# Latent queries of a two-layer block in three fp32r products, with five small moves of neighbouring work

## The chip, the cores and the metric

The kernel runs on one core of one Trainium2 chip, in one launch. The metric is the device time of one execution in microseconds (us). Three runs of the kernel before gave 2176.4, 2179.35 and 2181.2 us, so 2179.35 us in the median.

A core has TensorE (PE, matrix products, with its weight loads shown as PEld), VectorE (DVE), ScalarE (ACT), GpSimd (POOL) and SyncE (SP), which here only issues the DMA transfers. Each engine works through its own list in order, and the engines wait for each other by semaphores. Nothing is reordered at run time: an instruction that waits holds up all that stands behind it on its engine.

## The reference, cut to what matters

The program computes two transformer layers on 512 tokens of 1024 features. The parts that the change touches are these:

```python
x = x + rms_norm(mixed, post_norm_gain)                      # layer 1: a sum of squares over 1024 features ("post")
...
n = rmsnorm(h, norm_mix)                                     # layer 2: "mix", 528 tokens (16 more in front)
c_q = ...n @ w_in[:, 0:384]                                  # latent of the queries
q = (rmsnorm(c_q, q_norm) @ w_uq)                            # 384 -> 8 heads * (128 + 64): the latent queries
...
h = h + mix @ w_out
peer_ffn(rmsnorm(h, norm_ffn), ...)                          # "ffn"
    q = (h @ w_q);  s = q . sub_keys; top-k of 128 + 128 keys, 8 heads
    out[t] = sum over 16384 experts e of gate[t, e] * gelu(h[t] . u[e]) * v[e]
```

The expert layer is computed densely: all 16384 experts for all tokens, with a table of gates that is zero except for the chosen ones.

## The kernel before, in words

Features lie on the partitions and tokens along the free dimension, in tiles of 128 features by 512 tokens. A product is one of two kinds. **fp32 products** (`project`, line 791; sums of squares in `sums`, 884, and `big_sums`, 901) take the fp32 operands as they are; the trace shows each as two matmul records. **fp32r products** (`three`, lines 802 to 804) split both operands into an upper part, rounded to fp32r, and a lower part, the rest, and add up*up + up*low + low*up: three matmul records.

Weights come by DMA in chunks of up to 128x2048 into a ring of four slots of `wring`; the list WEIGHTS gives their order, and its last field says whether a chunk is to be split. POOL does the splitting (`split_group`): CASTs of 128x512 for the upper part (line 2577, one of two slots behind the ring) and subtractions for the lower part (line 2581, in place). It takes the chunks in the order of the list, waits for a chunk to land, and waits until the products of the chunk two places earlier in the list of split ones have released their upper slot. The order on each engine is written out by hand.

**Sums of squares.** For "post", "mix" and "ffn" ACT squares pairs of tiles, DVE adds the two tiles of a pair (`add_squares`, line 2002), and PE multiplies each of the four pair sums by a matrix of ones (line 901).

**Latent queries.** PE computes c_q, c_kv and k_pe, then 12 tiles of queries with 3 products of 128x512 each (`project_part`), in groups between sums of squares of earlier parts. The chunks are uqn0, uqn1 and uqp, 128x1536 each, not split.

**Expert scores and top-k.** For each of 8 heads PE computes the query (`query(h)`, weights pq0 to pq7) and then the scores (`ps`, line 1377), one head ahead. DVE finds the top-k (`best16`); POOL weighs the one-hot places (`weigh_places`, line 2613), DVE sums them. For pq6 and pq7 ACT does the rounding (line 1852), and POOL only the subtraction.

**First expert stage** (u). 128 tiles of 128 experts. A tile of 512 KB lands in one of six slots of `wring`; ACT rounds it (`round_u`, 1856), POOL makes the rest (`split_u`, 2621), PE does 16 products (1386, 1387), ACT takes the gelu (1878). ACT rounds tile t+4 behind the gelu of tile t. Beside tiles 44 to 111 the gate table is made in 128 quads: DVE makes one-hots (2494, 2495), ACT and POOL weigh them (1888, 2643), PE multiplies (1412, 1413) into PSUM, and DVE copies 128x512 to a stage (2504), from which SP stores the pieces to `gate_table`.

**Second expert stage** (v). 64 steps: ACT rounds v (`round_v`, 1893), DVE makes its rest (2509), DVE multiplies hidden values by gates (2519), ACT rounds these coefficients (1899), DVE makes their rest (2525), PE does 32 products (1438, 1439).

Of the kernel before, what the change touches and what calls it, by code (L numbers as in the profile page):

```python
# [80 lines left out]
USLOT = (1, 2, 3, 5, 0, 4)  # L81
# [39 lines left out]
for _name, _n in (("pre", 8), ("mix", 8), ("subln", 1), ("conv", 12), ("post", 8), ("ple", 8), ("qnorm", 3),  # L121
# [179 lines left out]

ADDED = ["post", "mix", "ffn"]


def build(nc, A):
    ctx = ExitStack()
    with ctx:
# [87 lines left out]
        cq = view(15488, 3, T)  # L395
        ckv = view(17024, 2, TM)
# [118 lines left out]
        x2_ready = sem("x2_ready")  # L515
        roped = sem("roped")
# [109 lines left out]
        def _(sp):  # L626
# [90 lines left out]
            for t in range(TILES):  # L717
# [13 lines left out]
                if t == TILES - len(USLOT) - 1:  # L731
# [3 lines left out]
                    load_v(1)  # L735

# [29 lines left out]
        def _(pe):  # L766
# [121 lines left out]
            def big_sums(name, width=T, pairs=range(4)):  # L888
# [5 lines left out]
                for m in pairs:  # L894
                    if name in ADDED:
                        pe.wait_ge(pair_added, 4 * ADDED.index(name) + m + 1)
                    else:
                        pe.wait_ge(squares, 4 * BIG.index(name) + m + 1)
                    for k in (2 * m,) if name in ADDED else (2 * m, 2 * m + 1):
                        for at, n in ((0, T), (T, META)) if width == TM else ((0, T),):  # L900
                            mm = pe.matmul(flat(key)[:, at:at + n], ones, sq[:, k, at:at + n],
                                           start=(k == 0), stop=(m == 3 and k == (6 if name in ADDED else 7)))
# [197 lines left out]

            def project_part(name):
                kind, m = name[0:2], int(name[2:])
                if kind == "qn":
                    if m == 0:
                        pe.wait_ge(normed, NORM["cq"] + 1)
                    project(("uqn", m), f"uqn{m // 2}", (2 * (m % 2), 2 * (m % 2) + 1), cq, 3)
                elif kind == "qp":
                    project(("uqp", m), "uqp", (2 * m, 2 * m + 1), cq, 3)
# [354 lines left out]
        def _(act):  # L1463
# [185 lines left out]
            square("ckv", norm_sq("ckv")[:, 0:2 * TM].rearrange("p (k t) -> p k t", k=2), ckv)  # L1649
            when_filled(act, ("kpe", 0))  # L1650
# [208 lines left out]
            for h in range(HP):  # L1859
                if h + 1 < HP:  # L1860
                    query(h + 1)
                copy_out(("ps", h), sc[:, h].rearrange("p a b -> p (a b)"), flat(("ps", h)))
                if h == HP - 2:
                    round_u(0)
                    round_u(1)
# [60 lines left out]
            for g in range(BEFORE + BESIDE, GROUPS):  # L1926
                for j in range(EG):
                    gelu(g, j)
                    beside(EG * g + j)
                    if g >= GROUPS - 2 and j % 2:  # L1930
                        if (g, j) == (GROUPS - 2, 1):
                            act.wait_ge(stored[1], 8 * PIECES * STORES)
                        round_v(2 * (g + 2 - GROUPS) + j // 2)
            for n in range(2):
                round_coefs(n)
            round_coefs(2)
# [861 lines left out]
```

## Time and profile before

| what | value |
|---|---|
| median of three runs | 2179.35 us (2176.4 to 2181.2) |
| the profiled execution's own time | 2177.73 us |
| its span, first to last instruction | 2175.9 us |
| PE busy | 2115.4 us, 97% |
| DVE, ACT, POOL busy | 1304.1, 922.6 and 1033.5 us |
| mean granted TensorE clock | 0.992 |

How to read it: the times below are those of the profiled execution, counted from the span's start; 1.8 us of its time lie outside the span. A matmul record lasts longer than the step to the next one because matmuls are pipelined; the step from start to start is what a product takes in a row of products.

### The profile page before, as it was taken

What the parts mean: (1) busy time and instruction counts of PE and PEld (TensorE: products, weight loads), DVE (VectorE), ACT (ScalarE), POOL (GpSimd) and SP (SyncE); (2) the same over time, 40 slices, a digit from 0 to 9 for tenths busy, and PEclk for the clock granted to TensorE, in tenths of its full rate; (3) what the DMA queues carried; (4) which work ended last, traced back from release to release, by engine and by line L of the source; (5) the groups of instructions that cost most, each with busy time, mean ns of one, the idle gap of its engine ahead of it and who ended that gap; (6) DMA issues with size and microseconds to landing.
All of it is one profiled execution on the core that took longest, in us unless ns stands there. A gap on an engine that the chain in (4) does not pass through costs nothing.

```text
span 2175.9 us, 27394 instructions
## 1 busy us (share of the span) xinstructions
PE 2115.4 (97%) x10296; PEld 1661.6 (76%) x10296; DVE 1304.1 (60%) x2244; ACT 922.6 (42%) x1528; POOL 1033.5 (47%) x892
## 2 busy tenths in 40 slices
PE   8999999999999999999999998999999899999999
PEld 6877767557887776887878877777778788888887
DVE  6456257352235774215898957888881666666664
ACT  4223343572234234111334447777773434343432
POOL 6655546212324122877859887999996100000000
PEclk9999999999999999999999999999999999999999
DMA  5222312201111111233216664777788988888884
GB/s 201 100 78 78 116 61 90 90 30 49 59 40 59 59 55 43 97 122 110 78 59 199 205 206 141 272 289 246 272 291 294 333 300 286 289 284 300 288 287 149
DMA packets 98291, 359.32 MB, mean 165 GB/s; under 512 B 8480, under 2 KB 41504, under 8 KB 73328
## 3 DMA queue, kind: packets, MB, share of 16 engines
q1 hardware_dynamic: 98160, 357.56, 47.3%
q8 instruction: 83, 1.36, 0.3%
q14 instruction: 48, 0.39, 0.1%
HBM read 286.09 MB, written 71.30 MB: 164 GB/s over the span
## 4 chain that ended last, share of the span: by engine, by line
PE 67%; POOL 13%; DVE 11%; issue 6%; ACT 2%; DMA 1%; POOLq 0%; SPq 0%; ACTq 0%; DVEq 0%
PE ps L1438 11%; PE ps L1439 11%; PE ps L802 10%; PE ps L803 9%; PE ps L804 9%; POOL area L2643 6%; POOL wring_parts L2621 6%; PE ps L791 2%; PE ps L1249 2%; DVE area L2413 2%; PE ps L1386 1%; PE ps L1387 1%; DVE area L2410 1%; PE ps L884 1%; PE ps L1225 1%
## 5 line engine op out<-in xcount | busy, mean ns | idle before, releaser
L2577 POOL CAST wring_parts<-wring 128x512 fp32r<-128x512 f32 x236 | 170.5, 764 | 546.0 <-PE ps L804 429.3
L1386 PE MATMUL ps<-sqbuf_parts,wring_parts 128*128 128x512 f32 x1024 | 412.6, 403 | 5.5 <-POOL wring_parts L2621 5.5
L1387 PE MATMUL ps<-normed_x_parts,wring_parts 128*128 128x512 f32 x1024 | 404.4, 395 | 0.0
L2621 POOL TENSOR_TENSOR wring_parts<-wring_parts,wring 128x512 fp32r<-128x512 f32 x256 | 331.0, 1323 | 76.0 <-ACT wring_parts L1856 73.0
L2581 POOL TENSOR_TENSOR wring_parts<-wring,wring_parts 128x512 fp32r<-128x512 f32 x244 | 351.2, 1470 | 6.6 <-ACT wring_parts L1852 1.5
L1386 PEld LDWEIGHTS ps<-sqbuf_parts,wring_parts 128*128 128x128 f32 x1024 | 194.0, 189 | 50.6 <-POOL wring_parts L2621 4.9
L1387 PEld LDWEIGHTS ps<-normed_x_parts,wring_parts 128*128 128x128 f32 x1024 | 193.9, 189 | 41.8
L802 PE MATMUL ps<-resid_parts,wring_parts 128*128 128x512 f32 (+1 forms) x528 | 201.2, 381 | 6.1 <-DVE normed_x_parts L2010 3.3
L803 PE MATMUL ps<-normed_x_parts,wring_parts 128*128 128x512 f32 (+1 forms) x528 | 197.0, 373 | 0.0
L804 PE MATMUL ps<-resid_parts,wring_parts 128*128 128x512 f32 (+1 forms) x528 | 196.2, 372 | 0.0
L1474 ACT ACTIVATE area<-ps 128x1024 f32<-128x1024 f32 (+6 forms) x89 | 61.7, 696 | 275.2 <-PE ps L804 183.5
L2504 DVE COPY area<-ps 128x512 f32<-128x512 f32 x128 | 138.9, 1087 | 56.3 <-PE ps L1413 56.3
L803 PE MATMUL ps<-area_parts,wring_parts 128*128 128x512 f32 x440 | 172.4, 392 | 0.0
L1888 ACT ACTIVATE area<-area,rt 128x128 bf16<-128x128 bf16 x512 | 156.5, 390 | 3.7 <-DVE area L2494 3.7
L1878 ACT ACTIVATE area<-ps 128x512 f32<-128x512 f32 x128 | 76.3, 597 | 187.0 <-PE ps L1387 187.0
L802 PE MATMUL ps<-area_parts,wring_parts 128*128 128x512 f32 x376 | 150.1, 399 | 4.8 <-POOL wring_parts L2581 2.3
L804 PE MATMUL ps<-area_parts,wring_parts 128*128 128x512 f32 x376 | 146.7, 390 | 0.0
L1438 PE MATMUL ps<-cst_parts,area_parts 128*128 128x512 f32 x352 | 138.3, 393 | 4.7 <-issue 4.7
L1439 PE MATMUL ps<-rt_parts,area_parts 128*128 128x512 f32 x352 | 138.0, 392 | 0.0
L1856 ACT ACTIVATE wring_parts<-wring 128x1024 fp32r<-128x1024 f32 x128 | 134.4, 1052 | 7.2 <-DMA wring<-in_uT_dram 7.2
L1438 PE MATMUL ps<-normed_x_parts,area_parts 128*128 128x512 f32 x352 | 136.9, 389 | 0.0
L1439 PE MATMUL ps<-normed_x_parts,area_parts 128*128 128x512 f32 x352 | 136.9, 389 | 0.0
(269 smaller groups left out, 4431.4 us busy)
## 6 DMA issues: line engine op xcount, KB each, us to landing
wring<-in_weights_dram SPq DMA_DIRECT2D x65, 1024.0 KB, 4.8
wring<-in_uT_dram SPq DMA_DIRECT2D x128, 512.0 KB, 4.4
area<-in_vT_dram SPq DMA_DIRECT2D x44, 1024.0 KB, 7.2
hidden_table<-area SPq DMA_DIRECT2D x32, 1024.0 KB, 6.7
gate_table<-area SPq DMA_DIRECT2D x32, 1024.0 KB, 8.4
area<-gate_table SPq DMA_DIRECT2D x32, 1024.0 KB, 9.1
wring<-in_vT_dram SPq DMA_DIRECT2D x20, 1024.0 KB, 6.7
rt<-hidden_table SPq DMA_DIRECT2D x32, 512.0 KB, 4.6
```

The lines of the kernel that those rows point to most:

```text
L802: pe.matmul(out, a_up, b_up, start=first, stop=False)
L803: pe.matmul(out, a_up, b_low, start=False, stop=False)
L804: return pe.matmul(out, a_low, b_up, start=False, stop=last)
L1386: pe.matmul(out, first[:, d], h_first[:, k, :], start=(k == 0), stop=False)
L1387: mm = pe.matmul(out, rest[:, d], h_rest[:, k, :], start=False, stop=(k == KD - 1))
L1438: pe.matmul(out, v_first[:, j, d], c_first[:, t], start=(n == 0 and j == 0), stop=False)
L1439: mm = pe.matmul(out, v_rest[:, j, d], c_rest[:, t], start=False, stop=(n == HALVES - 1 and j == 1))
L1888: ins = act.activation(gateB[:, q, i, 0, :], oneB[:, q, i, :], ACT.Copy, scale=entT[:, 2, t:t + 1])
L2504: dve.tensor_copy(dst[:, 4 * i:4 * i + 4, :], spread_out(n)).then_inc(copied, 1)
L2577: ins = nc.gpsimd.tensor_copy(up[:, d, :], W(name)[:, d, :])
L2581: ins = nc.gpsimd.tensor_tensor(low[:, d, :], W(name)[:, d, :], up[:, d, :], ALU.subtract)
L2621: ins = nc.gpsimd.tensor_tensor(rest[:, a:a + PIECE], first[:, a:a + PIECE], u_raw[t % len(USLOT)][:, a:a + PIECE], ALU.subtract)
```

## The change

Six edits.

1. The chunks uqn0, uqn1 and uqp are split, so POOL gets nine CASTs and nine subtractions of 128x512 more. ACT rounds the normed latent c_q (128x1536) and DVE subtracts, and the 36 fp32 products of the queries become 108 fp32r products. As the list of split chunks is three longer, the upper slots swap, and the order of the u slots (USLOT) follows.
2. DVE adds the sums of the first three pairs into one tile, so that "post", "mix" and "ffn" need two products with ones in place of four. DVE gets two additions more for each.
3. The copy of a quad (line 2504) goes through the same elements in another order: it reads PSUM at a step of 128 elements and writes runs of four.
4. ACT rounds the u tiles 0 and 1 ahead of taking out the last query, and POOL splits them ahead of `weigh_places(1)` and of the subtraction of pq7; POOL splits tiles 2 and 3 ahead of `weigh_places(2)`, as before.
5. The loads of v 0 and 1 stand at tile 116 in place of 121.
6. ACT rounds v 2 and 3 behind the first two coefficients in place of between the last gelus, and DVE makes the rest of coefficient 1 ahead of v 2 and 3.

```diff
-USLOT = (1, 2, 3, 5, 0, 4)
+USLOT = (1, 2, 3, 4, 0, 5)
-              ("kpe0", 8, 128, True), ("uqn0", 3, 512, False), ("uqn1", 3, 512, False), ("uqp", 3, 512, False),
+              ("kpe0", 8, 128, True), ("uqn0", 3, 512, True), ("uqn1", 3, 512, True), ("uqp", 3, 512, True),
 ADDED = ["post", "mix", "ffn"]
+ADDED_TILES = ((), (), (4,), (6,))
...
-                if t == TILES - len(USLOT) - 1:
+                if t == EG * (BEFORE + BESIDE) + 4:
                     sp.wait_ge(stored[0], 8 * PIECES * STORES)
                     load_v(0)
                     load_v(1)
+                if t == TILES - len(USLOT) - 1:
...
                     if name in ADDED:
-                        pe.wait_ge(pair_added, 4 * ADDED.index(name) + m + 1)
+                        if m >= 2:
+                            pe.wait_ge(pair_added, 2 * ADDED.index(name) + m - 1)
...
+            def project_query(key, name, tiles):
+                claim(key)
+                up, low = split_arrived(name)
+                for a, m in enumerate(tiles):
+                    d = slice(m * P, (m + 1) * P)
+                    for k in range(3):
+                        mm = three(pair(key)[:, a, :], (up[:, k, d], low[:, k, d]),
+                                   (CQ_PARTS[0][:, k, :], CQ_PARTS[1][:, k, :]), k == 0, k == 2)
+                fills(mm, key)
...
-                        pe.wait_ge(normed, NORM["cq"] + 1)
-                    project(("uqn", m), f"uqn{m // 2}", (2 * (m % 2), 2 * (m % 2) + 1), cq, 3)
+                        pe.wait_ge(latent_low, 1)
+                    project_query(("uqn", m), f"uqn{m // 2}", (2 * (m % 2), 2 * (m % 2) + 1))
...
             square("ckv", norm_sq("ckv")[:, 0:2 * TM].rearrange("p (k t) -> p k t", k=2), ckv)
+            act.wait_ge(normed, NORM["cq"] + 1)
+            act.activation(CQ_PARTS[0], cq, ACT.Copy).then_inc(latent_up, 1)
...
             for h in range(HP):
+                if h == HP - 2:
+                    round_u(0)
+                    round_u(1)
                 if h + 1 < HP:
                     query(h + 1)
                 copy_out(("ps", h), sc[:, h].rearrange("p a b -> p (a b)"), flat(("ps", h)))
-                if h == HP - 2:
-                    round_u(0)
-                    round_u(1)
...
-                    if g >= GROUPS - 2 and j % 2:
-                        if (g, j) == (GROUPS - 2, 1):
-                            act.wait_ge(stored[1], 8 * PIECES * STORES)
-                        round_v(2 * (g + 2 - GROUPS) + j // 2)
+                    if g == GROUPS - 2 and j % 2:
+                        round_v(j // 2)
             for n in range(2):
                 round_coefs(n)
+            act.wait_ge(stored[1], 8 * PIECES * STORES)
+            round_v(2)
+            round_v(3)
...
-                dve.tensor_tensor(sq[:, 2 * m, :], sq[:, 2 * m, :], sq[:, 2 * m + 1, :], ALU.add).then_inc(pair_added, 1)
+                ins = dve.tensor_tensor(sq[:, 2 * m, :], sq[:, 2 * m, :], sq[:, 2 * m + 1, :], ALU.add)
+                if m in (1, 2):
+                    link(ins)
+                    ins = dve.tensor_tensor(sq[:, 2 * m, :], sq[:, 2 * m, :], sq[:, 2 * m - 2, :], ALU.add)
+                if m < 2:
+                    link(ins)
+                    return
+                ins.then_inc(pair_added, 1)
...
+            dve.wait_ge(latent_up, 1)
+            dve.tensor_tensor(CQ_PARTS[1], cq, CQ_PARTS[0], ALU.subtract).then_inc(latent_low, 1)
...
-                dst = stage[:, piece % 2, :].rearrange("p (j t) -> p t j", t=HALF)
+                dst = stage[:, piece % 2, :].rearrange("p (j t) -> p j t", t=HALF)
                 dve.wait_ge(spread, n + 1)
-                dve.tensor_copy(dst[:, 4 * i:4 * i + 4, :], spread_out(n)).then_inc(copied, 1)
+                dve.tensor_copy(dst[:, :, 4 * i:4 * i + 4], spread_out(n).rearrange("p t n -> p n t")).then_inc(copied, 1)
...
             split_coefs(0)
+            split_coefs(1)
             split_v(2)
             split_v(3)
-            split_coefs(1)
...
             for h in range(HP):
-                if h == 2:
-                    for split in range(4):
+                if h in (1, 2):
+                    for split in range(2 * h - 2, 2 * h):
                         split_u(split)
                 weigh_places(h)
```

Three places show how instructions move. Line numbers of the changed kernel are some 5 to 31 higher. First POOL, at the end of the weight chunks: 2613 and 2644 are `weigh_places`, 2581 and 2612 the subtraction of a query chunk (pq6, then pq7), 2621 and 2652 `split_u`. Before:

```order
L2613 TENSOR_TENSOR area<-area 128x1024 [waits places_hot] x2
L2581 TENSOR_TENSOR wring_parts<-wring,wring_parts 128x512 [waits query_up,filled0,w_in3]
L2581 TENSOR_TENSOR wring_parts<-wring,wring_parts 128x512 x3
L2613 TENSOR_TENSOR area<-area 128x1024 [waits places_hot] x2
L2581 TENSOR_TENSOR wring_parts<-wring,wring_parts 128x512 [waits query_up,filled2,w_in0]
L2581 TENSOR_TENSOR wring_parts<-wring,wring_parts 128x512 x3
L2621 TENSOR_TENSOR wring_parts<-wring_parts,wring 128x512 [waits u_rounded]
L2621 TENSOR_TENSOR wring_parts<-wring_parts,wring 128x512
```

And of the change:

```order
L2644 TENSOR_TENSOR area<-area 128x1024 [waits places_hot] x2
L2612 TENSOR_TENSOR wring_parts<-wring,wring_parts 128x512 [waits query_up,filled0,w_in3]
L2612 TENSOR_TENSOR wring_parts<-wring,wring_parts 128x512 x3
L2652 TENSOR_TENSOR wring_parts<-wring_parts,wring 128x512 [waits u_rounded]
L2652 TENSOR_TENSOR wring_parts<-wring_parts,wring 128x512
L2652 TENSOR_TENSOR wring_parts<-wring_parts,wring 128x512 [waits u_rounded]
L2652 TENSOR_TENSOR wring_parts<-wring_parts,wring 128x512
L2644 TENSOR_TENSOR area<-area 128x1024 [waits places_hot] x2
L2612 TENSOR_TENSOR wring_parts<-wring,wring_parts 128x512 [waits query_up,filled2,w_in0]
L2612 TENSOR_TENSOR wring_parts<-wring,wring_parts 128x512 x3
```

Two `split_u`, each waiting for ACT's rounding, now stand ahead of `weigh_places(1)` and pq7.

Second ACT at the same place: 1474 and 1493 are copies out of PSUM (query 6, scores 5, query 7, scores 6, scores 7), 1856 and 1877 `round_u`. Before:

```order
L1474 ACTIVATE area<-ps 128x1024 [waits filled0,filled3]
L1474 ACTIVATE area<-ps 128x1024 [waits filled1]
L1474 ACTIVATE area<-ps 128x1024 [waits filled2,filled1]
L1474 ACTIVATE area<-ps 128x1024 [waits filled3]
L1856 ACTIVATE wring_parts<-wring 128x1024 [waits u_in0]
L1856 ACTIVATE wring_parts<-wring 128x1024 [waits u_in1]
L1474 ACTIVATE area<-ps 128x1024 [waits filled0]
```

And of the change:

```order
L1493 ACTIVATE area<-ps 128x1024 [waits filled0,filled3]
L1493 ACTIVATE area<-ps 128x1024 [waits filled1]
L1877 ACTIVATE wring_parts<-wring 128x1024 [waits u_in0]
L1877 ACTIVATE wring_parts<-wring 128x1024 [waits u_in1]
L1493 ACTIVATE area<-ps 128x1024 [waits filled2,filled1]
L1493 ACTIVATE area<-ps 128x1024 [waits filled3]
L1493 ACTIVATE area<-ps 128x1024 [waits filled0]
```

The two roundings moved up by two copies and still stand behind the copy of scores 5.

Third the transfers that SP issues near the end of the first expert stage. Before:

```order
L680 DMA hidden_table<-area 128x2048 [waits gelu_done]
L676 DMA wring<-in_uT_dram 128x1024 [waits pre_done] x4
L680 DMA hidden_table<-area 128x2048 [waits gelu_done]
L676 DMA wring<-in_uT_dram 128x1024 [waits pre_done]
L694 DMA area<-in_vT_dram 128x2048 [waits stored0]
L694 DMA area<-in_vT_dram 128x2048
L700 DMA area<-gate_table 128x8x256 [waits spread,stored1]
```

And of the change:

```order
L685 DMA hidden_table<-area 128x2048 [waits gelu_done]
L699 DMA area<-in_vT_dram 128x2048 [waits stored0]
L699 DMA area<-in_vT_dram 128x2048
L681 DMA wring<-in_uT_dram 128x1024 [waits pre_done] x4
L685 DMA hidden_table<-area 128x2048 [waits gelu_done]
L681 DMA wring<-in_uT_dram 128x1024 [waits pre_done]
L705 DMA area<-gate_table 128x8x256 [waits spread,stored1]
```

The two loads of v, 1 MB each, now stand ahead of the last five u tiles (123 to 127).

## Rows read from the trace of the kernel before

**Rows 1.** The page, part 1: busy us, share of span, instructions.
```profile
PE 2115.4 (97%) x10296; PEld 1661.6 (76%) x10296; DVE 1304.1 (60%) x2244; ACT 922.6 (42%) x1528; POOL 1033.5 (47%) x892
```
**Rows 2.** Waits of PE, longest first: us in total, times, longest us.
```profile
PE ps L1412 <- POOL area L2643: 10.4, 26, 2.4
PE ps L1386 <- POOL wring_parts L2621: 5.5, 5, 2.9
```
**Rows 3.** Timeline of PE, an fp32r stretch: start us, us, engine and line.
```profile
235.18 0.39 PE L804 MATMUL ps<-area_parts,wring_parts 128*128 128x512 f32 x1
...
244.28 0.39 PE L804 MATMUL ps<-area_parts,wring_parts 128*128 128x512 f32 x1
```
**Rows 4.** Chain that ended last, latent queries: start us, us, what.
```profile
397.39 5.15 PE ps L791 x12
...
403.62 15.65 PE ps L791 x36
```
**Rows 5.** Timeline of ACT and POOL ahead of the latent queries.
```profile
390.50 1.09 ACT L1482 ACTIVATE sqbuf<-area 128x1056 f32<-128x1056 f32 x1
381.47 1.17 POOL L2577 CAST wring_parts<-wring 128x512 fp32r<-128x512 f32 x2 [6.17 <-PE ps L804]
```
**Rows 6.** Timeline of DVE in "mix": the same subtraction beside POOL and alone.
```profile
343.95 2.31 DVE L1984 TENSOR_TENSOR area_parts<-area,area_parts 128x1024 fp32r<-128x1024 f32 x1
354.82 1.23 DVE L1984 TENSOR_TENSOR area_parts<-area,area_parts 128x1024 fp32r<-128x1024 f32 x1 [0.51 <-ACT area_parts L1508]
```
**Rows 7.** Timeline of PE, products with ones in post, mix, ffn.
```profile
281.64 3.60 PE L901 MATMUL ps<-sqbuf,cst 128*128 128x512 f32 x8
354.37 1.25 PE L901 MATMUL ps<-sqbuf,cst 128*128 128x512 f32 x4 [1.08 <-DVE sqbuf L2002]
1033.23 1.02 PE L901 MATMUL ps<-sqbuf,cst 128*128 128x512 f32 x2
```
**Rows 8.** Windows of PE: length, busy (instructions), PEclk, DMA share, GB/s.
```profile
986.30:990.30 4.00, 2.17 (x10) 1.00 0.05 20
444.60:448.60 4.00, 2.04 (x7) 0.87 0.00 0
1137.30:1145.30 8.00, 8.00 (x29) 0.80 0.19 52
1145.30:1153.30 8.00, 8.00 (x36) 1.00 0.47 147
```
**Rows 9.** Timeline of ACT, PE, POOL around query 7 and tile 0.
```profile
1118.55 1.02 ACT L1474 ACTIVATE area<-ps 128x1024 f32<-128x1024 f32 x1 [0.70 <-PE ps L1377]
1119.61 0.47 PE L802 MATMUL ps<-area_parts,wring_parts 128*128 128x512 f32 x1 [1.09 <-POOL wring_parts L2581]
1137.29 0.76 PE L1386 MATMUL ps<-sqbuf_parts,wring_parts 128*128 128x512 f32 x1 [2.94 <-POOL wring_parts L2621]
```
**Rows 10.** Timeline of POOL in the same stage.
```profile
1088.27 4.73 POOL L2613 TENSOR_TENSOR area<-area 128x1024 f32<-128x1024 f32 x2
1094.47 5.03 POOL L2581 TENSOR_TENSOR wring_parts<-wring,wring_parts 128x512 fp32r<-128x512 f32 x4 [1.47 <-ACT wring_parts L1852]
1134.64 9.98 POOL L2621 TENSOR_TENSOR wring_parts<-wring_parts,wring 128x512 fp32r<-128x512 f32 x8 [15.17 <-ACT wring_parts L1856]
```
**Rows 11.** Line 2504: min/median/max ns, first and last start.
```profile
L2504 DVE COPY area<-ps x128: 1001/1086/1115, 1313.8 to 1641.1; 128x512 f32<-128x512 f32 x128
```
**Rows 12.** Waits of DVE from 1340 to 1640 us.
```profile
DVE area L2504 <- PE ps L1413: 45.3, 62, 2.0
```
**Rows 13.** Timeline of ACT, PE and DVE, end of the first expert stage.
```profile
1670.99 1.06 ACT L1856 ACTIVATE wring_parts<-wring 128x1024 fp32r<-128x1024 f32 x1
1678.14 8.20 DMA area<-in_vT_dram
1706.36 0.76 PE L1438 MATMUL ps<-cst_parts,area_parts 128*128 128x512 f32 x1 [4.74 <-issue]
1705.04 1.23 DVE L2525 SCALAR_TENSOR_TENSOR rt_parts<-cst_parts,rt 128x1024 fp32r<-128x1024 f32 x1 [5.08 <-ACT cst_parts L1899]
```

More of the change, by code:

```diff
@@ L395, in build @@
         cq = view(15488, 3, T)
+        CQ_PARTS = [area_parts[:, at:at + 3 * T].rearrange("p (k t) -> p k t", k=3) for at in (10368, 15488)]
         ckv = view(17024, 2, TM)
@@ L515, in build @@
         x2_ready = sem("x2_ready")
+        latent_up = sem("latent_up")
+        latent_low = sem("latent_low")
         roped = sem("roped")
@@ L895, in big_sums @@
                     if name in ADDED:
-                        pe.wait_ge(pair_added, 4 * ADDED.index(name) + m + 1)
+                        if m >= 2:
+                            pe.wait_ge(pair_added, 2 * ADDED.index(name) + m - 1)
                     else:
                         pe.wait_ge(squares, 4 * BIG.index(name) + m + 1)
-                    for k in (2 * m,) if name in ADDED else (2 * m, 2 * m + 1):
+                    for k in ADDED_TILES[m] if name in ADDED else (2 * m, 2 * m + 1):
                         for at, n in ((0, T), (T, META)) if width == TM else ((0, T),):
                             mm = pe.matmul(flat(key)[:, at:at + n], ones, sq[:, k, at:at + n],
-                                           start=(k == 0), stop=(m == 3 and k == (6 if name in ADDED else 7)))
+                                           start=(k == ADDED_TILES[2][0] if name in ADDED else k == 0),
+                                           stop=(k == ADDED_TILES[3][0] if name in ADDED else k == KD - 1))
                 if pairs[-1] == 3:
@@ L1104, in project_part @@
                     if m == 0:
-                        pe.wait_ge(normed, NORM["cq"] + 1)
-                    project(("uqn", m), f"uqn{m // 2}", (2 * (m % 2), 2 * (m % 2) + 1), cq, 3)
+                        pe.wait_ge(latent_low, 1)
+                    project_query(("uqn", m), f"uqn{m // 2}", (2 * (m % 2), 2 * (m % 2) + 1))
                 elif kind == "qp":
-                    project(("uqp", m), "uqp", (2 * m, 2 * m + 1), cq, 3)
+                    project_query(("uqp", m), "uqp", (2 * m, 2 * m + 1))
                 else:
```

## The prediction, made before the change was run

> **What bounds the kernel now.** I read the page's first part, then the waits of PE, then the timeline of each stage that the diff touches. PE is busy 97% of a span of 2175.9 us [rows 1], so an edit shows in the time only where it shortens PE's own work or one of its few waits, or makes a new wait. In the list of waits the reader is to see how little there is to win: the largest entry is 10.4 us in 26 pieces behind POOL's weighing of one-hots, the next 5.5 us behind the splitting of u [rows 2]. The timelines then tell, per edit, whether PE waits there, and for which instruction. A second thing to watch is the granted clock. After 1.83 us without work PE kept full clock, and after 1.96 us and 2.94 us it did not (0.87 and 0.80 in the windows behind) [rows 8, 9]. The full-clock window of 8 us holds 36 products, the one behind the 2.94 us holds 29 [rows 8]: 7 to 8 products of 0.23 us, about 1.7 us lost. So a wait of over about 2 us costs itself and some 1.7 us more, and a wait that gets shorter than that gives both back.
>
> **The sums of squares** (edit 2). In "post" eight records (four products) take 3.60 us, the last one's pipelined end included [rows 7], so 0.86 us each. PE does not wait there, and two products go: -1.7. DVE's two added adds (0.7 us each by the size of such adds, my estimate) lie beside earlier products. In "mix" two products of about 1.1 us (1.25 with the pipelined end) [rows 7] go too, but PE already waited 1.08 us for DVE's add of the last pair before 354.37. That add comes no earlier, so the 2.1 us turn into idle time, 3.2 us in all, which passes the 2 us after which the clock fell: no gain and one half-clock episode, +1.6, between 0 and +1.8. In "ffn" the last product stands at 1033.23 [rows 7]; the addition that it needs ends about 0.6 us before, so it can move up by 0.5: -0.5, between -1.7 and 0.
>
> **The latent queries** (edit 1). 36 records of fp32 take 15.65 us [rows 4]; two records are a product, so a product takes 0.869 us. An fp32r product in three records: from 235.18 to 244.28 the stretch holds 13 of them, 9.10 us [rows 3], 0.700 each. 36 products: 36 x 0.169 is -6.1, with the same from a second stretch -6.2. What must be ready in time: PE reaches the first of them at 397.39 [rows 4]. ACT is free at 391.59 [rows 5] and takes about 1.5 us for 128x1536 (1.09 for 1056), so 393.1. DVE's subtraction of 1024 columns took 2.31 us beside POOL and 1.23 alone [rows 6]; for 1536 that is 1.8 to 3.5, so 394.9 to 396.6. POOL casts at 0.58 us and subtracts at 1.25 us per 512 [rows 5, 10], 5.5 us for a chunk of 1536; free from 389.8 on, it would have the first chunk at about 396.5 at the latest, the second at 402, the third at 412 to 414, where PE wants them at 397, 407 and 420. So covered, with a slack under a microsecond for the first: -6.2, at worst -5.2 (1 us of wait). If POOL were wholly late by a chunk's 5.5 us, -0.7; I don't take that as an end since it was idle 6.17 us in that place [rows 5].
>
> **The order around query 7** (edit 4). This is the term that decides. Before, POOL did `weigh_places(1)` (4.73 us) and the subtraction of pq7 (5.03 us) [rows 10] while PE did scores 5, and PE waited only 1.09 us for it before query 7 at 1119.61 [rows 9]. Now two `split_u` stand ahead of both, and each waits for a rounding that ACT does behind its copy of scores 5. That copy starts only when PE has finished scores 5, at 1118.55, and ends at 1119.57 [rows 9]. So POOL is held from about 1100 to: round_u(0) done 1120.6; splits 0 and 1, 2 x 2.5 (9.98 us for four tiles [rows 10]), 1125.6; weigh_places 4.73, 1130.3; subtraction 5.03, 1135.4; query 7 at about 1135.6. PE has nothing else in its order: +16.0. Behind 17 us of idle it runs at half clock, +1.7. Given back: tiles 0 and 1 are split early, so the wait of 2.94 us before tile 0 [rows 9] becomes about 1.15 us (now for ACT's copy of the last scores), -1.8, and no half clock there, -1.6. DVE's top-k chain behind `weigh_places(1)` is late by only some 9.7 us against PE's 16, so POOL's weighing in the stage after, on which PE waits in small pieces [rows 2], is earlier against PE by about 6 us; some 1.3 us of these waits lie in its first part and I take them off. Sum: 16.0 + 1.7 - 1.8 - 1.6 - 1.3 = +13.0, between +11 and +17.
>
> **The end of the first expert stage** (edits 5 and 6). Before, the load of v 0 was issued at 1678.14 and took 8.20 us [rows 13]; ACT, which rounds v 0 between the last gelus, stood still for it, PE waited about 1.1 us in two pieces behind that, and its second stage then started at 1706.36 after 4.74 us without work, for DVE's rest of the coefficient (1.23 us, ending 1706.27) [rows 13]. With v 0 early, the first stage ends 1.1 to 1.7 us sooner, and ACT goes straight from the last gelu to the coefficients; its 5.08 us ahead of DVE [rows 13] shrink to the rounding itself. I get coefficients at 1701.5, their rest at 1702.9, the second stage at 1703: -3.4, with 3.1 us still idle, so the half clock stays. Lower end -1 (only the 1.1 us). The price could be in the u tiles 123 to 127, issued behind these 2 MB. At the 400 GB/s of a full queue (1 MB in some 2.6 us, my estimate; a queue's share alone was 8.20 us [rows 13]) they come about 5.2 us later; tile 123 was rounded at 1670.99 [rows 13] and PE reads it only some 10 us later, so 1.2 us of slack are left by my count. I take 0 for it.
>
> **The quad copy** (edit 3). It takes 1.086 us now, 128 times [rows 11]. DVE was idle 45.3 us at just these copies, waiting for PE [rows 12]: over some 118 quads 0.38 us each, so a copy of up to 1.47 us costs nothing, and a faster one gains nothing unless it loosens a wait of PE. The new access is in no row. Bounds: 0.61 us (the 1.225 us that other copies out of PSUM take for 1024, halved, my estimate) and twice the present, 2.17 us. The old copy goes through one side at a wide step already, the new one through the other, so I take the present value: 0.
> The Trainium skill, page "PSUM — Partial Sum Buffer", section "Specifications (TRN2)", gives PSUM lines of 8 bytes and says that patterns that are not contiguous slow access; "SBUF — State Buffer", section "Specifications (TRN2)", gives SBUF lines of 16 bytes of which two hits are wanted. By the first the new read is worse, by the second the new write of four fp32 in a row is better. No row here tells which wins.
>
> **Sum** over the profiled execution: -1.7 + 1.6 - 6.2 - 0.5 + 13.0 - 3.4 = +2.8, rounded up for the wait that may be left before the first query: +3.0, so 2177.7 + 3.0 = 2180.7. The profiled execution lies 1.6 us below the median of the runs; on the median it is 2182.4.
>
> **Rivals.**
> (a) Slower, the copy. Reading PSUM at a step of 128 elements costs DVE more than the 0.38 us of slack. It decides from 1.47 us on; at 2.17 us each quad sets the pace, (2.17 - 1.47) x 128 = +90, about 2270. For it: never seen here. Against it: a copy that reads in order and writes at a step costs 1.09 already.
> (b) Slower, the loads. The two v loads hold the five u tiles for the 8.20 us that one took in rows 13, not for 5.2: PE waits about 4.3 us for tile 123 and pays a half clock: +6, about 2188. For it: 8.20 us is the only duration of such a load in the rows. Against it: two loads were issued together there, beside u tiles. Of each SDMA engine the Trainium skill ("DMA: Bandwidth & Descriptors", section "Queues, rings and completion order") says that it takes descriptors in ring order, which would make the u tiles wait whole; the order on SP alone shows that too.
> (c) Faster, no hole. POOL or ACT get to tiles 0 and 1 early by a way that I have overlooked, and query 7 is not held. Then the waits before tile 0 go and nothing comes: -6.8 - 3.4 - 3.4 = -13.6 or a bit less, 2166. For it: ACT and POOL each have stretches without work in this stage, so the work itself would fit. Against it: the waits in the order leave no other way.
> (d) Faster copy. At 0.6 us, DVE releases PSUM and the stage earlier and some of the 10.4 us behind POOL [rows 2] go: +3.0 - 7 to 8, about 2175.
> (e) The clock is kinder: no episode in "mix", none behind the hole, and the one behind 1.96 us at 444.6 goes: 3.0 - 5, about 2177.
>
> **Chances.** Forecast 0.60, its own range 2178 to 2187; (a) 0.07, (b) 0.10, (c) 0.07, (d) 0.08, (e) 0.08. A measurement of this kernel can't tell under 0.2% from no change, that is 4.4 us, 2175.0 to 2183.7. Faster: (c) 0.07, half of (d) 0.04, 0.02 of the forecast and of (e) 0.01, so 0.14. Slower: (a) 0.07, (b) 0.07, the forecast 0.27: 0.41. Same: 0.45. The range goes down past (d) and up past (b), 2171 to 2191; it leaves out (a) and (c), 0.14, and tails.
>
> **What would show it.** PE idle of about 16 us before query 7, its releaser POOL's subtraction, and POOL idle ahead of a `split_u` that waits for ACT; no wait of PE at 397; the query stretch 25 us long, not 31; PE idle 3 us before the last product of "mix"; tile 0 started behind ACT; the second expert stage some 3 us earlier against the end of the first; the quad copy's mean under 1.4 us. I am wrong if query 7 is not late, if the copy's mean passes 1.47 us, or if PE waits for u tiles 123 to 127.

## The result: 0.2% slower, and the trace of the kernel after

| | before | after |
|---|---|---|
| median of 22 runs each | 2177.62 us | 2182.46 us |
| ratio of after to before | | 1.0022, 95% interval 1.0014 to 1.0029 |
| profiled execution: time, span | 2177.73, 2175.9 us | 2182.15, 2180.4 us |

The forecast was 2182.4 us with a difference of +3.0 us; measured were 2182.46 us and +4.8 us. That the time itself was hit to 0.1 us is luck in part: the three runs of before that I had lay 1.7 us above the median of 22, and the difference was 1.8 us too small.

I cut both profiled executions at PE instructions that stand in both (a start is the time in the timeline of PE) and compare the lengths of the pieces:

| piece, by its start in before | before, us | after, us | difference | forecast |
|---|---|---|---|---|
| up to 199.8 (nothing changed) | 199.82 | 199.23 | -0.6 | 0 |
| to 324.88: "post" | 125.06 | 123.32 | -1.7 | -1.7 |
| to 375.92: "mix" | 51.04 | 52.54 | +1.5 | +1.6 |
| to 446.67: latent queries | 70.75 | 64.82 | -5.9 | -6.2 |
| to 988.33 (nothing changed) | 541.66 | 541.70 | 0.0 | 0 |
| to 1118.52, scores 5 done: "ffn" | 130.19 | 129.77 | -0.4 | -0.5 |
| to 1341.64: hole at query 7 and what is given back | 223.12 | 237.96 | +14.8 | +13.0 |
| to 1706.36: quads, end of the first expert stage | 364.72 | 362.08 | -2.6 | -3.4 |
| to the end | 469.54 | 468.98 | -0.6 | 0 |
| sum | 2175.9 | 2180.4 | +4.5 | +2.8 |

The page's first part of after. PE lost 11 us of work and gained 16 us of idle time against [rows 1], POOL got 18 instructions more, DVE 26 us less work:

```profile
PE 2104.0 (96%) x10316; PEld 1666.4 (76%) x10316; DVE 1278.2 (59%) x2251; ACT 923.6 (42%) x1529; POOL 1052.0 (48%) x910
```

The waits of PE in after, longest first (us in total, times, longest us), answer to [rows 2]. A line that was 2.6 us in all is now at the top; the one for the rest of u has shrunk:

```profile
PE ps L808 <- POOL wring_parts L2612: 18.4, 3, 16.9
PE ps L1431 <- POOL area L2674: 10.7, 27, 2.3
...
PE ps L908 <- DVE sqbuf L2024: 4.5, 2, 3.5
...
PE ps L1457 <- issue: 2.9, 1, 2.9
...
PE ps L1405 <- POOL wring_parts L2652: 2.2, 3, 0.8
```

The timeline of after around query 7 (start us, us, instruction, idle time before it). Read it in time: ACT's copy of scores 5, its rounding of u 0 behind it, POOL idle for 21 us and then the two splits, the weighing, the subtraction of pq7, and PE 16.93 us without work:

```profile
1111.42 1.02 ACT L1493 ACTIVATE area<-ps 128x1024 f32<-128x1024 f32 x1 [0.70 <-PE ps L1396]
1112.34 1.05 ACT L1877 ACTIVATE wring_parts<-wring 128x1024 fp32r<-128x1024 f32 x1
1113.46 4.92 POOL L2652 TENSOR_TENSOR wring_parts<-wring_parts,wring 128x512 fp32r<-128x512 f32 x4 [21.10 <-ACT wring_parts L1877]
1118.35 4.64 POOL L2644 TENSOR_TENSOR area<-area 128x1024 f32<-128x1024 f32 x2
1122.94 5.22 POOL L2612 TENSOR_TENSOR wring_parts<-wring,wring_parts 128x512 fp32r<-128x512 f32 x4
1128.31 0.76 PE L808 MATMUL ps<-area_parts,wring_parts 128*128 128x512 f32 x1 [16.93 <-POOL wring_parts L2612]
1146.97 0.47 PE L1405 MATMUL ps<-sqbuf_parts,wring_parts 128*128 128x512 f32 x1 [1.31 <-ACT area L1493]
```

Against [rows 9, 10]: the wait of 1.09 us became 16.93, the 2.94 us before tile 0 became 1.31 behind ACT. Windows of PE (length, busy with instructions, clock, DMA share, GB/s) in after, behind the hole, behind the start of tile 0, from the last product of "mix" on and over the queries:

```profile
1128.30:1136.30 8.00, 7.99 (x24) 0.65 0.00 0
1147.00:1155.00 8.00, 8.00 (x35) 1.00 0.21 68
352.28:360.28 8.00, 8.00 (x27) 0.79 0.08 31
396.80:427.40 30.60, 30.60 (x126) 1.00 0.30 103
```

Behind the hole only 24 products fit in 8 us where 36 do at full clock [rows 8]: this episode cost 2.7 us, not the 1.7 that I took from the one behind 2.94 us. Tile 0 now starts at full clock. The queries take 30.6 us from the first to the product behind them; the same stretch of before is 397.39 to 434.28, 36.9 us.

What made the queries ready in after, and the last product of "mix", in the timeline:

```profile
390.97 1.47 ACT L1670 ACTIVATE area_parts<-area 128x1536 fp32r<-128x1536 f32 x1
391.18 5.29 POOL L2612 TENSOR_TENSOR wring_parts<-wring,wring_parts 128x512 fp32r<-128x512 f32 x3
392.47 2.86 DVE L2195 TENSOR_TENSOR area_parts<-area,area_parts 128x1536 fp32r<-128x1536 f32 x1 [2.99 <-ACT area_parts L1670]
396.61 0.48 PE L808 MATMUL ps<-area_parts,wring_parts 128*128 128x512 f32 x1
352.28 1.22 PE L908 MATMUL ps<-sqbuf,cst 128*128 128x512 f32 x1 [3.49 <-DVE sqbuf L2024]
```

POOL was done at 396.47 and DVE at 395.33, and PE's first query product starts at 396.61 without a wait (the record before it ends at 396.86): the cover was between 0.1 and 0.4 us thick. In "mix" the wait of 1.08 us in [rows 7] is 3.49 us.

The quad copy in after, against [rows 11, 12] (the line's min/median/max ns and first and last start; then DVE's wait from 1340 to 1640 us):

```profile
L2535 DVE COPY area<-ps x128: 673/690/694, 1322.0 to 1648.3; 128x512 f32<-128x512 f32 x128
```
```profile
DVE area L2535 <- PE ps L1432: 85.8, 62, 4.2
```

It got 0.40 us cheaper, 128 times, and DVE waits 40 us more for PE. The end of the first stage in after, against [rows 13]:

```profile
1671.14 1.06 ACT L1877 ACTIVATE wring_parts<-wring 128x1024 fp32r<-128x1024 f32 x1 [7.56 <-DMA wring<-in_uT_dram]
1674.86 0.50 PE L1405 MATMUL ps<-sqbuf_parts,wring_parts 128*128 128x512 f32 x1 [0.80 <-POOL wring_parts L2652]
1685.12 1.06 ACT L1877 ACTIVATE wring_parts<-wring 128x1024 fp32r<-128x1024 f32 x1 [5.66 <-DMA wring<-in_uT_dram]
1709.01 1.99 ACT L1920 ACTIVATE cst_parts<-rt 128x1024 fp32r<-128x1024 f32 x2
1710.09 2.36 DVE L2556 SCALAR_TENSOR_TENSOR rt_parts<-cst_parts,rt 128x1024 fp32r<-128x1024 f32 x2 [5.03 <-ACT cst_parts L1920]
1711.42 0.76 PE L1457 MATMUL ps<-cst_parts,area_parts 128*128 128x512 f32 x1 [2.94 <-issue]
```

ACT did wait 5.66 us for the first u tile behind the v loads, and PE did not wait for it. The tile with the 7.56 us was issued ahead of the v loads; there PE waited 0.80 us. Before had ACT's wait at that place too (6.54 us) but none of PE. PE's idle time before the second stage is 2.94 us instead of 4.74.

### The profile page after: what moved, and what is told of

It reads as the page before. It is cut to its first block, busy times and chain, and to the rows that moved or that the text cites. A ratio compares the mean times of both kernels' runs of the same rounds, so it can differ in the third digit from the quotient of the medians.

```text
span 2180.4 us, 27469 instructions
## 1 busy us (share of the span) xinstructions
PE 2104.0 (96%) x10316; PEld 1666.4 (76%) x10316; DVE 1278.2 (59%) x2251; ACT 923.6 (42%) x1529; POOL 1052.0 (48%) x910
## 3 DMA queue, kind: packets, MB, share of 16 engines
q8 instruction: 83, 1.36, 0.3%
## 4 chain that ended last, share of the span: by engine, by line
PE 70%; POOL 13%; DVE 9%; issue 6%; ACT 2%; DMA 1%; SPq 0%; POOLq 0%; ACTq 0%; DVEq 0%
PE ps L808 11%; PE ps L1457 11%; PE ps L1458 11%; PE ps L809 11%; PE ps L810 11%; POOL area L2674 6%; POOL wring_parts L2652 5%; PE ps L1268 2%; PE ps L1405 1%; PE ps L1406 1%; DVE area L2444 1%; PE ps L890 1%; PE ps L1244 1%; PE ps L797 1%; DVE area L2441 1%
## 5 line engine op out<-in xcount | busy, mean ns | idle before, releaser
L2608 POOL CAST wring_parts<-wring 128x512 fp32r<-128x512 f32 x245 | 177.7, 766 | 521.7 <-PE ps L810 439.0
L2612 POOL TENSOR_TENSOR wring_parts<-wring,wring_parts 128x512 fp32r<-128x512 f32 x253 | 362.2, 1461 | 6.8 <-ACT wring_parts L1873 1.5
L809 PE MATMUL ps<-area_parts,wring_parts 128*128 128x512 f32 x476 | 187.6, 394 | 0.0
L808 PE MATMUL ps<-area_parts,wring_parts 128*128 128x512 f32 x412 | 166.2, 403 | 20.1 <-POOL wring_parts L2612 18.1
L810 PE MATMUL ps<-area_parts,wring_parts 128*128 128x512 f32 x412 | 161.8, 393 | 0.0
L2535 DVE COPY area<-ps 128x512 f32<-128x512 f32 x128 | 87.7, 686 | 95.8 <-PE ps L1432 95.8
```

What stands on the lines that cost most here:

```text
L808: pe.matmul(out, a_up, b_up, start=first, stop=False)
L809: pe.matmul(out, a_up, b_low, start=False, stop=False)
L810: return pe.matmul(out, a_low, b_up, start=False, stop=last)
L2608: ins = nc.gpsimd.tensor_copy(up[:, d, :], W(name)[:, d, :])
L2612: ins = nc.gpsimd.tensor_tensor(low[:, d, :], W(name)[:, d, :], up[:, d, :], ALU.subtract)
```

## The experiments

Twelve kernels, in three groups of four. The median of before on the same chip was 2179.11 us for e1 to e4, 2179.59 us for e5 to e8 and 2179.81 us for e9 to e12. Ratios are to before, with their 95% interval.

**e1, edit 4 put back, the other five kept.**

```diff
             for h in range(HP):
-                if h == HP - 2:
-                    round_u(0)
-                    round_u(1)
                 if h + 1 < HP:
                     query(h + 1)
                 copy_out(("ps", h), ...)
+                if h == HP - 2:
+                    round_u(0)
+                    round_u(1)
...
-                if h in (1, 2):
-                    for split in range(2 * h - 2, 2 * h):
+                if h == 2:
+                    for split in range(4):
```

> The changed kernel with the order around query 7 (edit 4) put back on ACT and POOL; the other five edits stay. Theory (the wait of 16.9 us before query 7 comes from the two split_u ahead of weigh_places(1) and pq7, and nothing else in the change costs): PE waits under 1.5 us before query 7, 2.9 us before tile 0 with half clock behind it, and the time falls by about 14.5 us against the change, to some 10 us below the kernel before (2167 to 2169). Rival (the nine chunks more that POOL splits, or the early v loads, hold the stages behind, and the wait only hides it): the wait at query 7 goes, but 5 us or more of it come back later, so the time stays above 2172.

Measured: 2172.08 us, ratio 0.9966 (0.9953 to 0.9979), so 7.0 us under before by the medians and, by the two ratios, about 12 us under the change. The hole is gone, and as the rival said something came later. Three waits of PE in this kernel:

```profile
1111.67 0.47 PE L808 MATMUL ps<-area_parts,wring_parts 128*128 128x512 f32 x1 [1.06 <-POOL wring_parts L2612]
1129.33 0.47 PE L1405 MATMUL ps<-sqbuf_parts,wring_parts 128*128 128x512 f32 x1 [2.94 <-POOL wring_parts L2652]
1228.66 0.50 PE L1405 MATMUL ps<-sqbuf_parts,wring_parts 128*128 128x512 f32 x1 [3.60 <-POOL wring_parts L2652]
```

The third did not exist in before's trace. POOL's timeline shows what it waited for:

```profile
1220.50 5.66 POOL L2644 TENSOR_TENSOR area<-area 128x1024 f32<-128x1024 f32 x2 [6.07 <-DVE area L2497]
```

POOL stood 6.07 us in `weigh_places`, for one-hots that DVE's top-k makes, with u tiles queued behind. POOL's list there holds no chunk, and the v loads come 400 us later, so the rival's cause is wrong, though its effect is there. What held DVE is told behind the experiments: two slow operations, which stand in a trace of the kernel before (e10) too.

**e2, only POOL's half of edit 4 put back** (ACT still rounds u 0 and 1 early; the last four lines of the diff above).

> The changed kernel with only POOL's half of edit 4 put back: ACT still rounds u 0 and 1 ahead of copying query 7, POOL again does weigh_places(1) and pq7 first. Theory (POOL's order alone makes the hole; ACT's early rounding is good by itself): no wait over 1.5 us before query 7, tile 0 starts behind ACT's copy of the last scores after 1.2 to 1.5 us instead of 2.9 us and at full clock, so 2.5 to 3.5 us below the kernel with all of edit 4 put back, about 2165. Rival (ACT's two roundings, 2 us, delay its copy of query 7 or the rounding of pq7, on which PE waits): a new wait of 1 to 2 us before scores 7, no gain against that kernel.

Measured: 2164.74 us, ratio 0.9931 (0.9911 to 0.9950), 14.4 us under before. The difference to e1 is 7 us by the medians, with intervals that nearly touch; the trace shows 3 of them, tile 0 behind ACT as forecast, at full clock. The profiled execution (2169.13 us) is the slowest of its five, the others took 2162.6 to 2165.5 us:

```profile
1129.81 0.47 PE L1405 MATMUL ps<-sqbuf_parts,wring_parts 128*128 128x512 f32 x1 [1.31 <-ACT area L1493]
1279.46 0.79 PE L1405 MATMUL ps<-sqbuf_parts,wring_parts 128*128 128x512 f32 x1 [3.59 <-POOL wring_parts L2652]
```

The second row is the same late wait as in e1, at another head.

**e3, edit 4 alone on the kernel before** (the diff of e1 read the other way).

> The kernel before with edit 4 alone. Theory: a wait of 16 to 17 us before query 7, half clock behind it, tile 0 early; the time is 13 to 15 us above the kernel before (2191). Rival (the hole needs POOL to be later through the other edits): under 8 us above.

Measured: 2192.34 us, ratio 1.0066 (1.0044 to 1.0087), +13.2 us by the medians. The wait is the same to the hundredth:

```profile
1132.64 0.76 PE L802 MATMUL ps<-area_parts,wring_parts 128*128 128x512 f32 x1 [16.93 <-POOL wring_parts L2581]
```

**e4, edit 1 alone on the kernel before** (the diff of edit 1 in the section on the change).

> The kernel before with edit 1 alone (latent queries in three fp32r products). Theory: 36 products at 0.70 instead of 0.87 us, all splitting covered: -6.2 us, no PE wait for POOL or DVE between 390 and 430 us. Rival (POOL's 18 instructions more or DVE's subtraction are late at 397 us): a wait of 1 to 5 us there and a gain under 4 us.

Measured: 2173.76 us, ratio 0.9973 (0.9960 to 0.9985), -5.4 us. No wait of PE between 390 and 430 us. Its trace has the late wait of 3.60 us too, at 1201.30, so its time is not that of the queries alone.

**e5, weighing one tile later**, on the kernel of e2:

```diff
-                    for split in range(split + 1, split + 8):
+                    for split in range(split + 1, split + (9 if h == 2 else 8)):
```

> The kernel of e2 (the change with POOL's half of edit 4 put back), and weigh_places of heads 3 to 7 stands one u tile later in POOL's order. Theory (in e1, e2 and e4 one PE wait of 3.6 us came because POOL stood 6 us in weigh_places behind DVE's top-k, with u tiles queued behind it): no PE wait over 1 us for a u tile's rest between 1150 and 1300 us, 2.5 to 5 us below the kernel of e2. Rival (DVE needs the weighed places so early that it stands instead, and the gate table comes later): DVE waits for POOL before its sums, the wait moves to the first quads near 1320 us, no change or slower by 1 to 2 us.

Measured: 2161.35 us, ratio 0.9922 (0.9907 to 0.9937), 3.4 us under e2. Between 1150 and 1300 us only one wait of PE is left, 0.71 us at 1276.28. The piece from tile 0 to the quad at which I cut took 207.8 us in e2 and 201.1 us here, but e2's trace has the late wait in it. In after, which has the old place of the weighing, a tile 0 at full clock and no late wait, it took 202.4 us: so the traces show at most 1.3 us for the order itself. DVE's idle times ahead of its sums of the weighed places are the same three in both (0.6, 2.3 and 1.1 us), so the rival's cost did not come.

**e6, "mix" in four products again**, on the kernel of e2:

```diff
                     if name in ADDED:
-                        if m >= 2:
+                        if name == "mix":
+                            pe.wait_ge(pair_added, 2 + m + 1)
+                        elif m >= 2:
...
+                if name == "mix":
+                    ins.then_inc(pair_added, 1)
+                    return
                 if m in (1, 2):
```

> The kernel of e2 with the sums of squares of mix in four products again; post and ffn keep two. Theory (the two products saved in mix turn into a wait of 3.5 us, and the half clock behind it is pure loss): the wait before the last product is 1.1 us, PE's clock stays full there, the part from there on is 1.5 to 2 us earlier; 1.5 us below the kernel of e2. Rival (the two products are saved in the end, since PE was in the way of the pair's add or of what follows): same or 2 us slower than e2.

Measured: 2165.54 us, ratio 0.9937 (0.9921 to 0.9953): no difference to e2 that the time shows. The trace does, in windows of 8 us that begin at the last product with ones, e6 first and then e2:

```profile
352.60:360.60 8.00, 7.94 (x34) 1.00 0.20 64
```
```profile
352.90:360.90 8.00, 7.96 (x27) 0.79 0.09 35
```

The wait is 1.08 us again, the clock stays full, and from that product to PE's next long wait (2.76 us for DVE, at 374.20 and 375.70) it is 21.5 us in place of 22.8. So two products less cost 1.2 us here instead of saving 2; the median can't show that. The other traces bear it out: this stretch is 21.5 us in each of the eight kernels with four products and 22.8 to 24.1 us in the six with two. Their late waits differ as well, 1.75 us in e6 and 3.59 in e2.

**e7, both**, e5 and e6 together.

> The kernel of e2 with both changes, of e5 and of e6. Theory: the two gains add up, 4 to 6.5 us below the kernel of e2, about 2159. Rival (what PE gains at mix is given back behind DVE's top-k, since DVE sets the pace there): no better than the kernel of e5.

Measured: 2160.17 us, ratio 0.9918 (0.9903 to 0.9933): 19.4 us under before and, by the ratios, about 23 us under the change, the best of all. Against e5 it is 1.2 us, within the spread.

**e8, edits 5 and 6 alone on the kernel before** (their diffs stand in the section on the change).

> The kernel before with edits 5 and 6 alone (v 0 and 1 loaded at tile 116, v 2 and 3 rounded behind the first coefficients). Theory: the two waits of 0.56 us in the last u tiles go and the wait at the start of the second stage is 2.9 us instead of 4.7 us: -2.5 to -3.4 us. Rival (the v loads hold the u tiles 123 to 127): a PE wait of over 2 us between 1675 and 1700 us, same or slower.

Measured: 2177.02 us, ratio 0.9997 (0.9985 to 1.0008). The time doesn't show a gain. The piece from the quad at 1341.64 to the start of the second stage does: 361.2 us here, and 362.0 to 362.3 us in the seven other traces that have edits 5 and 6, against 364.0 to 365.3 us in the five without (before, e3, e4, e9, e12; e10 has another copy). PE's wait before the second stage:

```profile
1700.79 0.76 PE L1439 MATMUL ps<-cst_parts,area_parts 128*128 128x512 f32 x1 [2.94 <-issue]
```

The piece from there to the end, which nobody changed, varied from 467.6 to 470.5 us between these traces, as much as the gain.

**e9, edit 3 alone on the kernel before** (the two lines of the copy).

> The kernel before with edit 3 alone: the quad copy reads PSUM at a step of 128 elements and writes runs of four. In the changed kernel's trace it takes 0.69 us instead of 1.09. Theory (DVE had 0.38 us to spare per quad and PE's small waits behind POOL do not depend on the copy): 0.69 us, DVE idle 0.4 us more per quad, time within 2 us of the kernel before. Rival (the faster copy frees PSUM and loosens PE's 26 small waits behind POOL's weighing): 5 to 8 us faster.

Measured: 2178.05 us, ratio 1.0002 (0.9986 to 1.0017). The copy takes 0.687 us and PE's small waits are untouched:

```profile
L2504 DVE COPY area<-ps 128x512 f32<-128x512 f32 x128 | 87.8, 687 | 95.7 <-PE ps L1413 95.7
```
```profile
PE ps L1412 <- POOL area L2643: 10.2, 26, 2.2
```

**e10, the old copy twice**, on the kernel before:

```diff
+                link(dve.tensor_copy(dst[:, 4 * i:4 * i + 4, :], spread_out(n)))
                 dve.tensor_copy(dst[:, 4 * i:4 * i + 4, :], spread_out(n)).then_inc(copied, 1)
```

> The kernel before with each quad copy done twice, with the same operands. 2.17 us instead of 1.09 per quad. Theory (a copy above 1.47 us sets the pace of a quad): (2.17 - 1.47) x 128, some 90 us slower, PE waits for DVE in the quads. Rival (DVE's idle time is spread unevenly, so that it can't be used, or PE can run further ahead than I count): 1.09 x 128 = 139 us slower, or under 60 us.

Measured: 2254.22 us, ratio 1.0349 (1.0332 to 1.0365), +74.4 us or 0.58 us per quad. Two copies of 1.07 us are 2.14, so by a straight line the price begins at 1.56 us per quad; I had counted 1.47. DVE has no wait left from 1340 us on, so it sets the pace; PE's wait is still put down to POOL:

```profile
PE ps L1412 <- POOL area L2644: 82.1, 50, 2.8
```

**e11, the new copy twice**, on the kernel of e2 (the same edit on the new line).

> The kernel of e2 with each quad copy (in the new order) done twice. 1.37 to 1.45 us per quad, just under the 1.47 us from which I said a copy costs time. Theory: within 4 us of the kernel of e2 (2164.7). Rival (slack is less than I counted, since oneA and oneB of the next quads are late first): over 20 us slower.

Measured: 2167.55 us, ratio 0.9950 (0.9936 to 0.9963), 2.8 us over e2 with intervals that overlap. 1.37 us per quad are hidden, and DVE's wait in the quads falls to 5.2 us in 8 times.

**e12, edit 2 alone on the kernel before** (its diff stands in the section on the change).

> The kernel before with edit 2 alone (two products with ones instead of four in post, mix and ffn). Theory: post -1.7, mix +1.6 with a wait of about 3.3 us and half clock behind it, ffn -0.5: -0.6 us, not to be told from no change. In the trace: the wait before the last product of mix 3.2 to 3.5 us, PEclk below 0.85 in the 8 us behind it. Rival (the products saved count in full): -4 us.

Measured: 2178.69 us, ratio 0.9995 (0.9984 to 1.0007). The wait in "mix" is 3.48 us behind it only 21 products fit in 8 us, and the stretch that was 21.5 us in e6 is 24.1 us long:

```profile
352.98 2.32 PE L904 MATMUL ps<-sqbuf,cst 128*128 128x512 f32 x4 [3.48 <-DVE sqbuf L2006]
```
```profile
353.00:361.00 8.00, 8.00 (x21) 0.61 0.08 31
```

## Why the prediction was right, point by point

- **Sums of squares.** Right in all three: -1.7, +1.5, -0.4 against -1.7, +1.6, -0.5. e12 shows that together they are nothing in the time, and e6 that in "mix" the two products are better kept. The half clock behind a wait of 3.5 us has no fixed price: in the 8 us behind it stand 27 products in after, e2 and e5, and 21 to 23 in e1, e11 and e12.
- **Latent queries.** -5.9 in the trace and -5.4 in e4 against -6.2. The cover held, with 0.1 to 0.4 us to spare; DVE's subtraction took 2.86 us (bounds 1.8 to 3.5).
- **The order around query 7.** The mechanism was right link by link: 16.93 us of idle, +15.8 against +16.0 forecast, and the cause is POOL's order alone (e1, e2, e3). Two terms were mis-sized. The clock behind the hole cost 2.7 us, where I had put 1.7. And the -1.3 for POOL's weighing did not come at all: PE's waits between tile 0 and the quads are 1.36 us in after (the 1.31 ahead of tile 0 apart) and 1.43 in before, those of the first quads grew from 4.73 to 5.49 us (2.26, 0.39 and 2.84 in place of 2.30 and 2.43), and the line of waits for POOL's weighing went from 10.4 to 10.7 us. That the sum still came as near as +14.8 against +13.0 is luck: the granted clock over the first quads was 0.82 in after and 0.74 in before (1330.50 to 1349.34 and 1322.30 to 1341.64 us), which gave back about 1.1 us that nobody had counted.
- **The clock.** I had read 1.83 us without work as harmless and 1.96 as not, and put the border near 2 us. The traces don't bear a border out. The wait ahead of line 791 (at 446.67 us in before) stands in all of them (in e5 it is shorter, 1.41 us, and the clock stays full). Half clock followed 1.96 us in before, 2.00 in e7, 2.07 in after, 2.21 in e2 and 2.38 in e6; full clock followed 1.97 us in e4 and e10, 2.00 in e1, and 2.01 to 2.18 in e3, e8, e9, e11 and e12. Before and e3, the 8 us behind it:

```profile
446.67:454.67 8.00, 8.00 (x27) 0.79 0.00 0
447.23:455.23 8.00, 7.71 (x29) 1.00 0.01 2
```

- **The end.** -2.6 against -3.4; the second stage waits 2.9 us, as forecast (3.1), and the two waits of PE for v 0 are gone. These are 1.8 and 1.1 us; the rest of the piece was 0.3 us longer, with the wait of 0.80 us at 1674.86 in it. That wait comes with edit 1: it is 0.40 to 0.85 us in the eight traces that have the edit (0.85 in e4, which has nothing else), and no trace without it has one over 0.3 us there; I had not seen this cost. DVE's wait for ACT's coefficients did not shrink as I had written (5.03 us against 5.08). e8 gives -3.5 in the same piece.
- **The quad copy.** 0, as forecast. What I took for its duration was wrong by a third (0.69, not 1.09). Rival (a), a slower read, fell. What the Trainium skill says of PSUM's lines of 8 bytes ("PSUM — Partial Sum Buffer", section "Specifications (TRN2)"), that patterns which are not contiguous slow matmuls, I had carried over to DVE's reads; this trace does not bear that out; what it says of SBUF's lines of 16 bytes ("SBUF — State Buffer", section "Specifications (TRN2)") agrees with it, since the cheaper copy is the one that writes four fp32 in a row (0.69 against 1.09 us). Rival (d), a gain from a faster copy, fell with e9. e10 and e11 bracket the point at which the copy begins to cost between 1.37 and 2.14 us.
- **Rival (b), the loads.** Its first half happened: ACT waited 5.66 us for the first u tile behind the v loads, in e8, with edits 5 and 6 alone, 5.10, and in before not at all for that tile. PE did not wait for that tile, so it cost nothing.
- **Rival (c), no hole,** said 2166 for the change without it. e1, which is just that, gave 2172 with ACT's order of before and e2 2165 with the new one. What (c) had not seen is the late wait: 3.60 us in e1's trace and 28 products in place of 35 in the 8 us behind it, together some 5 us.

What makes the late wait is the slow DVE operation, and not time that PE gained ahead. From 1150 to 1300 us POOL waits for DVE once per head, in before and in after alike 1.49, 2.31, 3.00 and 3.00 us. In five traces one of these waits is 6.05 to 6.07 us and PE's wait behind it 3.6 (e1, e2, e4, e10, e11), in e6 they are 4.15 and 1.75 us; each time a single operation of the top-k (7.6 us, in e6 5.2) began 23 to 25 us ahead of PE's product. One of the five is e10, the kernel before with nothing changed ahead of the quads. Its timeline:

```profile
1174.38 15.07 POOL L2622 TENSOR_TENSOR wring_parts<-wring_parts,wring 128x512 fp32r<-128x512 f32 x12
1182.09 7.90 DVE L2441 TENSOR_TENSOR area<-area 128x256 f32<-128x256 f32 x2
1190.02 2.55 POOL L2622 TENSOR_TENSOR wring_parts<-wring_parts,wring 128x512 fp32r<-128x512 f32 x2 [0.58 <-ACT wring_parts L1856]
1198.63 5.66 POOL L2614 TENSOR_TENSOR area<-area 128x1024 f32<-128x1024 f32 x2 [6.07 <-DVE area L2466]
1206.80 0.80 PE L1386 MATMUL ps<-sqbuf_parts,wring_parts 128*128 128x512 f32 x1 [3.61 <-POOL wring_parts L2622]
```

Such operations, 5.2 to 11.5 us long, stand between 1140 and 1262 us in eight of the fourteen traces (e1, e2, e4, e6, e8, e9, e10, e11); before, after, e3, e5, e7 and e12 have none. They come with edit 1 (e4) and without it (e8, e9, e10), so they aren't the change's. The five near 1145 us (9.0 to 11.5 us long) are followed by no wait of PE over 0.92 us. In e2 (timeline of DVE, the same line, early and in front of the wait of 3.59 us):

```profile
1093.67 0.69 DVE L2472 TENSOR_TENSOR area<-area 128x256 f32<-128x256 f32 x2
...
1254.78 7.89 DVE L2472 TENSOR_TENSOR area<-area 128x256 f32<-128x256 f32 x2
```

The profile names no wait for them, but their place does say something. All eleven lie beside subtractions that POOL does without a break, four to nine of them, and end 0.28 us behind the end of one; with no subtraction beside it the operation takes 0.35 to 0.83 us, beside one 1.2 to 1.5 us, and then too it ends 0.2 to 0.3 us behind that subtraction. So DVE is held by POOL's row, as far as times can show it; no run moved POOL's work away to test it. Not settled is why DVE gets in behind one subtraction most times and behind four to nine at others.

Since e5's and e7's traces have no such operation, they can't say whether the weighing one tile later would cover the late wait.

## What to carry to other kernels

An engine that works through a fixed list is held by its first unready entry, so before moving an instruction forward ask when its input is ready, not when its output is wanted: two splits of 2.5 us each, put ahead of work that PE was waiting for, left PE 16.9 us without work because their input came after that work was due. Move the producer early and leave the consumer where it was, and the same idea gains (e2; 3 us by the trace). And where the bound engine has only small waits, removing work from it helps only if its operands come earlier too: in "mix" two products less made the kernel wait longer, at a lower clock.

## What the hardware showed that I had not expected

- The direction of a transposing copy by DVE from PSUM matters: reading at a step of 128 elements and writing runs of four took 0.69 us for 128x512, reading in order and writing single elements at a step 1.09 us.
- The half clock behind a wait costs a different amount in each execution: behind the same 3.5 us in "mix" 27 products in 8 us in three traces and 21 to 23 in three (34 in e6, behind 1.08 us, at full clock), and behind 16.93 us 24. Behind waits of 1.96 to 2.38 us at one place it came in five traces and stayed away in eight.
- Single DVE operations on 128x256 took 5.2 to 11.5 us in eight of fourteen executions, where their equals take 0.35 to 1.5: each stood beside four to nine POOL subtractions in a row and ended 0.28 us behind the end of one.
